# Group norms dealt out one product per step, and the latent norm ahead of the forget gate's running sums, in a two-block transformer kernel

## What is computed

```python
def first_block(x, ...):
    for l in range(2):
        (fq, fk, fv, fgate, cq, ckv, kr, sq, sk, sv, wq, wk, wv) = split(x @ w_in[l])
        log_f = log_sigmoid(fgate + fox_b_f[l])
        cum = cumsum(log_f, axis=1)                    # forget gate's running sums, 4 heads
        out_a = causal_softmax(fq, fk, fv, cum)        # "fox": logits + cum[t] - cum[s]
        q  = rmsnorm(cq, g_q) @ w_uq                   # "mla": latent norm, 256 wide
        kv = rmsnorm(ckv, g_kv) @ w_ukv                #        latent norm, 128 wide
        out_b = causal_softmax(q with rope, k with rope, v)
        out_c = stick_breaking(sq, sk, sv)             # "stick"
        out_d = sliding_window_sink_alibi(wq, wk, wv)  # "swa"
        mix = concatenate([out_a, out_b, out_c, out_d])  # 4 groups of 256 channels
        y = group_rmsnorm(mix, mix_g[l]) @ w_o[l]      # each group by its own rms
        x = layernorm(ALPHA * x + y, ...)
        f = (silu(x @ w_gate) * (x @ w_up)) @ w_down
        x = layernorm(ALPHA * x + f, ...)
    return x
```

## Time and profile before

| | |
|---|---|
| time, median of 3 runs | 3336.74 us (3334.49 to 3337.41) |
| time of the profiled execution | 3334.95 us |
| its span in the profile | 3333.2 us |
| TensorE busy | 3197.7 us, 96% |
| VectorE busy | 1551.8 us, 47% |
| ScalarE busy | 720.0 us, 22% |
| GpSimd busy | 1965.5 us, 59% |
| mean granted TensorE clock | 0.977 |
| the chain that ended last | PE 89%, DVE 6%, issue 3%, ACT 2%, DMA 1% |

### The profile page before, as it was taken

One profiled execution on the slowest core, in us unless ns is written; L12 is line 12 of the kernel. 1 busy time (PEld: TensorE's weight loads), 2 busy tenths in 40 slices (PEclk: granted clock), 3 DMA queues, 4 the chain that ended last, 5 costly groups with the idle time before them and its releaser, 6 DMA issues.

```text
span 3333.2 us, 44754 instructions
## 1 busy us (share of the span) xinstructions
PE 3197.7 (96%) x15314; PEld 2619.2 (79%) x15314; DVE 1551.8 (47%) x1978; ACT 720.0 (22%) x1460; POOL 1965.5 (59%) x1566
## 2 busy tenths in 40 slices
PE   8988999989989999699999999999999999899998
PEld 7767888877768888588888668888888887588886
DVE  7577332285764231644326664432344236764422
ACT  3353110043522110411101331110111102421110
POOL 6323766653236666377766536776677666267763
PEclk9999999999989999899999999999999999899999
DMA  4111322221112232122233212222222332122221
GB/s 169 50 39 51 101 96 99 95 90 58 39 51 83 98 97 95 53 97 97 95 99 108 81 45 95 94 98 98 96 94 95 100 111 89 39 89 97 98 95 63
DMA packets 82021, 286.43 MB, mean 86 GB/s; under 512 B 9531, under 2 KB 13020, under 8 KB 81628
## 3 DMA queue, kind: packets, MB, share of 16 engines
q1 hardware_dynamic: 76032, 275.81, 25.0%
q10 hardware_dynamic: 5852, 8.78, 0.8%
HBM read 280.89 MB, written 3.67 MB: 85 GB/s over the span
## 4 chain that ended last, share of the span: by engine, by line
PE 89%; DVE 6%; issue 3%; ACT 2%; DMA 1%; DVEq 0%; ACTq 0%
PE bank_v L419 18%; PE bank_v L421 18%; PE bank_v L420 18%; PE bank_a L419 9%; PE bank_a L420 9%; PE bank_a L421 9%; PE bank_v L656 1%; PE bank_a L613 1%; PE bank_s L795 1%; PE bank_s L466 1%; PE bank_s L674 1%; ACT resid L992 1%; PE bank_v L636 0%; PE bank_a L458 0%; PE bank_s L682 0%
## 5 line engine op out<-in xcount | busy, mean ns | idle before, releaser
L393 POOL TENSOR_TENSOR w_lo<-raw,w_hi 128x1024 fp32r<-128x1024 f32 x520 | 1319.6, 2538 | 41.7
L390 POOL TENSOR_TENSOR zero<-zero 128x1 f32<-128x1 f32 x520 | 128.2, 246 | 1290.5 <-PE bank_v L421 960.4
L419 PE MATMUL bank_v<-xn_hi,w_hi 128*128 128x512 f32 (+1 forms) x1552 | 594.4, 383 | 8.9 <-DVE resid L1392 4.5
L421 PE MATMUL bank_v<-xn_hi,w_lo 128*128 128x512 f32 (+1 forms) x1552 | 585.9, 377 | 0.0
L420 PE MATMUL bank_v<-xn_lo,w_hi 128*128 128x512 f32 (+1 forms) x1552 | 585.8, 377 | 0.0
L419 PE MATMUL bank_a<-xn_hi,w_hi 128*128 128x512 f32 (+1 forms) x1360 | 523.6, 385 | 39.2 <-DVE xn_lo L1364 21.5
L391 POOL CAST w_hi<-raw 128x1024 fp32r<-128x1024 f32 x520 | 551.9, 1061 | 0.0
L420 PE MATMUL bank_a<-xn_lo,w_hi 128*128 128x512 f32 (+1 forms) x1360 | 518.5, 381 | 0.0
L421 PE MATMUL bank_a<-xn_hi,w_lo 128*128 128x512 f32 (+1 forms) x1360 | 518.2, 381 | 0.0
L419 PE MATMUL bank_v<-h_hi,w_hi 128*128 128x512 f32 (+1 forms) x1100 | 419.7, 382 | 0.0
L421 PE MATMUL bank_v<-h_hi,w_lo 128*128 128x512 f32 (+1 forms) x1100 | 418.6, 381 | 0.0
(11 more groups left out here) (328 smaller groups left out, 3409.4 us busy)
## 6 DMA issues: line engine op xcount, KB each, us to landing
raw<-in_w_stream SPq DMA_DIRECT2D x520, 512.0 KB, 3.3
rope<-in_rope ACTq DMA_DIRECT2D x2, 1024.0 KB, 5.0
da_v<-t_rows ACTq DMA_DIRECT2D x2, 1024.0 KB, 5.8
out<-resid SPq DMA_DIRECT2D x4, 512.0 KB, 2.7
t_rows<-t_row ACTq DMA_DIRECT2D x1, 1536.0 KB, 5.7
resid<-in_x SPq DMA_DIRECT2D x4, 256.0 KB, 3.5
resid<-in_x ACTq DMA_DIRECT2D x4, 256.0 KB, 8.9
mla_v<-in_alibi ACTq DMA_DIRECT2D x2, 512.0 KB, 5.8
```

Of the source, the lines that this page charges most:

```text
L390: pool.tensor_tensor(zero[:, 1:2], zero[:, 0:1], zero[:, 0:1], ALU.add)
L393: pool.tensor_tensor(w_lo[:, u, :], raw[:, u, :], w_hi[:, u, :].bitcast(F32), ALU.subtract).then_inc(*w_split.done(("unit", u)))
L419: pe.matmul(out, lhs_hi, rhs_hi, start=first, stop=False)
L421: return pe.matmul(out, lhs_lo, rhs_hi, start=False, stop=last)
```

## The change

Two parts, in both passes of the first block.

**The group norms of groups 0 and 1** are dealt out. TensorE makes `mix_row(0)` in step 27 and `mix_row(1)` in step 28, behind the scores and turned blocks of that step. VectorE makes one of the four products in each of the steps 28 to 31 (`mix_apply_chunk`). The rounding on ScalarE moves to steps 32 and 33, the rests on VectorE to steps 34 and 35. Of group 2, the variance moves from step 30 to 32, the root from ahead of step 32's work to behind step 33's, and the diagonals from step 32 to 34. VectorE's copy of a finished pair's values out of its bank moves to the end of the step.

**The latent norm** on VectorE, from the variance to the diagonals, goes ahead of the forget gate's chain. The scan writes `cum` directly, so the copy goes. `cum_lo` and the rows of `aug_k` go behind the rests of the latents, and on ScalarE `aug_q` goes behind the rounding of the latents.

```diff
@@ TensorE, attention()
-                    if n == ROWS_STEP:
-                        for g in range(EARLY_ROWS):
-                            mix_row(g)
+                    if 0 <= n - ROWS_STEP < EARLY_ROWS:
+                        mix_row(n - ROWS_STEP)
@@ ScalarE, attention()
-                    if n == len(STREAM):
-                        mix_root(2, 1)
...
-                    if n == ROWS_STEP + 1:
+                    if n == len(STREAM):
                         act.wait_ge(*w_used.after(("wq", 1)))
-                        for g in range(EARLY_ROWS):
-                            mix_hi_of(g)
+                        mix_hi_of(0)
+                    if n == len(STREAM) + 1:
+                        mix_root(2, 1)
+                        mix_hi_of(1)
@@ ScalarE, layer1
+                for n in range(3):
+                    act.wait_ge(*value.after(("lat", n)))
+                    split_hi("lat", n, cq[:, n, :], lat_hi)
                 act.wait_ge(*dve_step.after("cum_lo"))
                 act.wait_ge(*dve_step.after("aug_zero"))
                 for h in range(4):
...
-                for n in range(3):
-                    act.wait_ge(*value.after(("lat", n)))
-                    split_hi("lat", n, cq[:, n, :], lat_hi)
@@ VectorE, attention()
-                    if pair_ending_at(n - TURN_LAG - 2):
-                        tag, p = pair_ending_at(n - TURN_LAG - 2)
-                        keep((tag, "out", p), sums, qmix[:, OUT_CHUNK[tag] + p, :])
...
-                    if n == ROWS_STEP + 1:
-                        for g in range(EARLY_ROWS):
-                            mix_apply(g)
-                        for g in range(EARLY_ROWS):
-                            mix_lo_group(g)
-                    if n == len(STREAM) - 2:
+                    if 0 <= n - APPLY_STEP < 2 * EARLY_ROWS:
+                        mix_apply_chunk(n - APPLY_STEP)
+                    if n == len(STREAM):
                         mix_variance(2, 1, a_read.after("stick"))
-                    if n == len(STREAM):
+                    if n == len(STREAM) + 2:
+                        mix_lo_group(0)
                         mix_diagonals(2, 1)
+                    if n == len(STREAM) + 3:
+                        mix_lo_group(1)
+                    if pair_ending_at(n - TURN_LAG - 2):
+                        tag, p = pair_ending_at(n - TURN_LAG - 2)
+                        keep((tag, "out", p), sums, qmix[:, OUT_CHUNK[tag] + p, :])
@@ VectorE, layer1
-                dve.wait_ge(*act_step.after("f_ln"))
-                step(dve.scalar_tensor_tensor(... log_f ...), "log_f")
-                step(dve.memset(work[0:4, 0, :], 1.0), "log_ones")
-                step(dve.tensor_tensor_scan(work[0:4, 3, :], ...), "cum0")
-                step(dve.tensor_copy(cum[0:4, :], work[0:4, 3, :]), "cum")
-                step(dve.tensor_copy(as_r(work[0:4, 2, :]), cum[0:4, :]), "cum_hi")
-                step(dve.tensor_tensor(work[0:4, 3, :], ...), "cum_lo")
-                for r, part in ((0, 2), (64, 3)):
-                    ins = dve.tensor_scalar(aug_k[r + 32:r + 36, :], ...)
                 dve.wait_ge(*sums.after(("lat", "sum", 2)))
...
                 inverse("lat", 2, lat_diag)
+                dve.wait_ge(*act_step.after("f_ln"))
+                step(dve.scalar_tensor_tensor(... log_f ...), "log_f")
+                step(dve.memset(work[0:4, 0, :], 1.0), "log_ones")
+                step(dve.tensor_tensor_scan(cum[0:4, :], ...), "cum")
+                step(dve.tensor_copy(as_r(work[0:4, 2, :]), cum[0:4, :]), "cum_hi")
                 keep(("fk", 1), w_used, fox_k[:, 1, :])
...
                 for n in range(3):
                     split_lo("lat", n, cq[:, n, :], lat_hi, lat_lo)
+                step(dve.tensor_tensor(work[0:4, 3, :], ...), "cum_lo")
+                for r, part in ((0, 2), (64, 3)):
+                    ins = dve.tensor_scalar(aug_k[r + 32:r + 36, :], ...)
```

More of the change, by code:

```diff
@@ L90 @@
 ROWS_STEP = 27
+APPLY_STEP = 28
 OUT_CHUNK = dict(fox=0, mla=2, stick=4, swa=6)
@@ L1726, in _ @@
                 inverse("lat", 2, lat_diag)
+                dve.wait_ge(*act_step.after("f_ln"))
+                step(dve.scalar_tensor_tensor(out=work[0:4, 2, :], in0=work[0:4, 0, :], scalar=0.0,
+                                              in1=work[0:4, 1, :], op0=ALU.min, op1=ALU.subtract), "log_f")
+                step(dve.memset(work[0:4, 0, :], 1.0), "log_ones")
+                step(dve.tensor_tensor_scan(cum[0:4, :], work[0:4, 0, :], work[0:4, 2, :], 0.0,
+                                            ALU.mult, ALU.add), "cum")
+                step(dve.tensor_copy(as_r(work[0:4, 2, :]), cum[0:4, :]), "cum_hi")
                 keep(("fk", 1), w_used, fox_k[:, 1, :])
@@ L1734, in _ @@
                     split_lo("lat", n, cq[:, n, :], lat_hi, lat_lo)
+                step(dve.tensor_tensor(work[0:4, 3, :], cum[0:4, :], work[0:4, 2, :], ALU.subtract), "cum_lo")
+                for r, part in ((0, 2), (64, 3)):
+                    ins = dve.tensor_scalar(aug_k[r + 32:r + 36, :], work[0:4, part, :], -1.0, None, ALU.mult)
+                ins.then_inc(*dve_step.done("aug"))
                 for tile in (1, 3):
```

31 lines of the change are left out of this document (14 added, 17 removed).

## The result

The changed kernel took 3315.91 us (median of four runs, 3312.94 to 3317.91), against 3337.07 us for the kernel before (four runs): a ratio of 0.9937, with a 95% interval from 0.992 to 0.9954. The forecast was 3310.7 us, in a range of 3305 to 3321. Faster was right, and the time lies in the range, but about 21 us were gained where the sum said 26.

A forecast was written before the change was run, and what follows sets the result against it. TensorE, busy 96%, was taken as the bound, with token sums waiting on ScalarE's copies (13.0 us) and the latent spread on VectorE's diagonals (6.2 us). 1.1 + 6.6 + 9.2 + 9.2 = 26.1 us gained gave 3310.7 us, range 3305 to 3321.

The forecast's parts named there:

- Latent norm, second pass: From fk1's last product to fv's second: 8.96 us should become 2.33 with diagonals ahead of the gate chain, 6.6 us gained.
- Latent norm, first pass: Same stretch in the first pass: 3.45 us with a wait of 1.12 us in it, 1.1 us gained.
- The margin is about 0.5 us ... I take 0: VectorE's copy of fk1, behind the moved chain, ends about 0.5 us before fv needs its banks; cost taken as 0.
- The bound kept for the range: Latent norm: one slower step costs 1.2 us, 0.7 beyond the margin, per pass; 1.4 us kept for the range.
- a new wait of 2 us or more ... before fv: Sign against the prediction: such a wait before fv, in steps 30 to 34 or at `mix_row(2)` would prove it wrong.
- The stop: TensorE's 6.00 us wait before stick's token sums shrinks to 1.1: 4.9 us gained per pass, plus 0.8 at second `mix_row`.
- The clock behind the stop: Stick's token sums to the last value products: 7.7 us at low clock become 4.05 at full clock, 3.6 gained per pass.
- the clock stays low: Rival, group norms: small waits keep TensorE's clock low, 3.6 us per pass not gained; 3319 us, chance 0.09.
- clock above 0.9 in that stretch: Expected sign: TensorE's clock above 0.9 from `mix_row(0)` to swa's token sums, but for the last steps.
- Steps 31 to 34: Ring of maxima, exponentials, scaling and copies, 7.1 us in the first pass: change about even, 0, at worst 0.7 lost.
- the wait re-forms: Rival: 0.7 us of product in each of four steps adds to the ring, 2.8 us lost per pass; 3316 us, chance 0.07.
- Not slower: Answers the rival that TensorE stays at half clock into the output projection: 3349 us at 15 us of it, chance 0.02.

The follow-up runs named there:

- changed_again: The changed kernel itself, unaltered, measured once more on the same chip: 3314.05 us (3312.59 to 3318.01), ratio 0.9939.
- waits_filled: The changed kernel with idle products in TensorE's small waits, five in step 29 and five, two and two in steps 32 to 34: 3313.13 us, ratio 0.9928.
- chain_split: The changed kernel with the forget gate's chain cut in two, scan and `cum_hi` moved behind the latents' rests: 3311.95 us, ratio 0.9926.
- subtraction_in_quarters: The changed kernel with each of GpSimd's weight subtractions issued as four instructions of 256 columns: 3317.58 us, ratio 0.9942.

## Why the prediction was right, and where its sizes were off

The terms by the two profiled executions: forecast 1.1 + 6.6 + 9.2 + 9.2 = 26.1 us; measured −0.5 + 5.0 + 7.5 + 9.0 = 21.0 us. The rest of the 22.0 us between the two spans the edits don't explain: 0.6 and 0.5 us lost at the start and between the passes, and all that follows the second pass's sums 2.1 us shorter.

- **What bounded the kernel** was read rightly: both waits that it named went, 6.2 us at the spread and 9.4 of 13.0 us at the token sums, and the time followed. One of the two came back in another form, 4.0 us on fk1's copy.
- **Latent norm, second pass: 6.6 forecast, 5.0 measured.** The stretch to fv's second product gave 4.2 us. Another 0.8 came because fv runs at the full pace from its first product (0.28 us each instead of 0.42), which the prediction had left out of the sum as "up to 1 us". fv's first copy on VectorE stands 13.46 us behind fk1's last product (751.40 − 737.94), where it was 18.48.
- **Latent norm, first pass: 1.1 forecast, 0.5 lost.** The step that failed in both is "The margin is about 0.5 us ... I take 0". The chain was added up from durations of the old places. In the second pass the diagonals took 7.47 us instead of 6.65, and from the gate's first step to `cum_hi` went 4.86 us instead of 2.69. That is 3.0 us over, 2.5 beyond the margin, and the wait is 2.42. In the first pass 0.85 and 1.35 us over make 2.2, 1.7 beyond the margin, and the wait is 1.63. The bound kept for the range, 1.4 us per pass, sized it as one slow step and an 0.5 us margin; it was several, since each step that meets GpSimd at work waits for it. By the prediction's own sign, "a new wait of 2 us or more ... before fv", this part of it was wrong in the second pass.
- **The stop: 4.9 us per pass forecast.** A wait of 1.28 us stayed where 1.1 was taken, so 4.7 gained, and the 0.8 us at the second `mix_row` came in full: `mix_row(0)` to the sums is 7.00 us instead of 12.79, 5.8 against 5.7.
- **The clock behind the stop: 3.6 us per pass forecast, 2.2 and 2.0 measured, and only 0.4 and 0.5 in the profiled execution of `changed_again`.** From the sums to the turn 4.05 us were expected, and it took 5.46 and 5.78, there 7.28 and 7.28. This is the term that was mis-sized most. The working "at full clock ... if the clock does not fall" had no middle: in the fastest execution the sums came back to full pace, the values did not. The rival *the clock stays low* was half true. What speaks in the prediction against it, 40 products at full pace in 2.40 us in the same kind of steps, was a poor witness: around them TensorE is busy 3.29 of 4 us in the changed kernel (216 to 220) and 4.00 in the next two windows, in the window of the small waits 2.71 (228 to 232). `waits_filled` shows the term was nearly right for a full clock: 4.26 us in both passes. The sign "clock above 0.9 in that stretch" did not come: it was 0.65 from 232 to 236.
- **Steps 31 to 34: 0 forecast, 0.2 us lost in the first pass** (7.09 to 7.31) **and 1.3 gained in the second** (7.91 to 6.65). Both have the same gain in them: the root and its table load no longer stand ahead of ScalarE's copy of item 30, and between the last two groups of turned blocks 1.52 us pass instead of 2.06. The prediction had called this exchange even. The rest is where the clock fell: in the first pass slower turns and scores cost 0.8 us, in the second they cost 0.7 less than before. The rival *the wait re-forms*, at 2.8 us a pass, did not come.
- **The second pass's 9.0 us beside the 9.2 forecast is luck**: the clock behind the sums gave 1.6 us less than its term, and steps 31 to 34 gave 1.3 that had no term. `mix_row(2)` and the products behind it lost 0.3 us in both passes instead of 0.1.
- **Not slower**: the output projection's opening is back at a clock of 1.00 from 248 on.

The cause of the new waits is tested: `chain_split` takes them away by moving the scan, and `subtraction_in_quarters` by shortening what it waits for. That with the small waits filled the clock holds is shown by both passes of one profiled execution and one of two passes of another; why the clock falls at one place in one execution and at another in the next stays open.

## What to carry to other kernels

A duration from a timeline holds for its moment: before adding up a moved chain, look whom each step met in its old place and whom it meets in its new one, above all VectorE beside GpSimd, and take a margin of 0.5 us in such a sum for none. When a step is moved ahead of a copy that frees a bank, move only what must come first: cutting the chain took away both waits, which neither order of the whole chain did. Where a long stop of TensorE is dealt out into small ones, expect the stop's time back, but of the low clock behind it half or less, and look at more than one execution before trusting a figure for it.

## What the hardware showed

VectorE and GpSimd exclude each other for whole instructions, not by sharing a rate, where VectorE's step goes from SBUF to SBUF. Beside a running GpSimd instruction, a VectorE step from SBUF to SBUF ended its own time less 0.13 us after it: the scan 1.07 us after (own time 1.20), the gate's first step 0.54 (0.67), roundings and copies of 4x512 0.27 and 0.28 (0.41). Steps that read a bank took the same beside GpSimd and without: fk1's copy 0.69 and 0.68 us, the scaling of the latents 2.06 us for three and 1.39 for two. A step that only writes was not held up either: the ones, a MEMSET of 4x512, took 0.48 us at 737.12, inside a subtraction. That a tile is small did not help: a step on 4 partitions could cost 2.65 us. One of the latent norm's diagonals takes 0.27 us at the least and 2.4 at the most, in one and the same kernel. With the subtraction in quarters VectorE's busy time fell by 15%, while GpSimd's rose by 18% (a quarter takes 0.72 us or more, the whole 2.40). The Trainium skill's page SBUF — State Buffer, in its section on SBUF's two separate sides, says that the pair of ports these two engines share is an exclusive lock, held for the whole instruction, with the other engine fully blocked; the trace agrees, with the 0.13 us met to within 0.02 in the cases above. The prediction did not weigh it.

TensorE's granted clock fell in windows that held no stop above 1.3 us: to 0.65 and 0.51, with TensorE busy 2.71 and 2.92 of 4 us in or just ahead of them. It stayed at 1.00 in an execution in which idle products brought these to 3.86 and 3.03. In another execution of the same changed kernel it was 0.50 behind the same 2.71. These runs don't tell what decides where it falls.
